# Residual and square ahead of the last weight split, in two output projections and two down projections of a two-layer decoder

## What is computed

```python
for i in range(DEPTH):
    shift, scale, gate = ada_modulation(c, ada_w[i, 0], ada_b[i, 0])
    h = rms_norm(x) * (1.0 + scale) + shift
    y = forgetting_attention(h, ...) if i % 2 == 0 else latent_attention(h, ...)   # ends in  o @ w_o
    x = x + gate * y
    shift, scale, gate = ada_modulation(c, ada_w[i, 1], ada_b[i, 1])
    h = rms_norm(x) * (1.0 + scale) + shift
    x = x + gate * conv_gated_mlp(h, ...)       # ends in  (silu(g) * v) @ w_out
return rms_norm(x) * final_g
```

## Time and profile before

| | |
|---|---|
| median of 3 runs | 1476.24 us (1476.23 to 1476.41) |
| the profiled execution's own time | 1478.92 us |
| its span in the profile | 1477.1 us, 19726 instructions |
| PE busy | 1358.3 us, 92% |
| DVE busy | 837.2 us, 57% |
| ACT busy | 581.3 us, 39% |
| share of engines in the chain that ended last | PE 78%, DVE 8%, issue 6%, ACT 5% |

### The profile page before, as it was taken

The page is one execution under the profiler, slowest core; times in us unless marked ns, Lnnn a source line. Parts: engine busy times, 40 slices in busy tenths (PEclk is TensorE's granted clock), DMA queues, the critical chain, the costliest instruction groups (busy, mean ns, idle before and its releaser), DMA issues.

```text
span 1477.1 us, 19726 instructions
## 1 busy us (share of the span) xinstructions
PE 1358.3 (92%) x6615; PEld 1052.0 (71%) x6615; DVE 837.2 (57%) x1396; ACT 581.3 (39%) x1042; POOL 7.6 (1%) x21
## 2 busy tenths in 40 slices
PE   5799999988999999999988788888879999999997
PEld 2577777655667677888875566666758888888885
DVE  2555666634655556653236578787456666764333
ACT  4444444422422323332223266665344444442222
POOL 2000000000000000000000000000000000000000
PEclk8899999988999999999998799999989999999998
DMA  9521222155466663333331111111213333333331
GB/s 345 187 79 55 58 58 57 30 171 185 168 222 244 223 242 99 99 92 93 94 105 35 22 28 29 30 30 57 71 43 100 99 99 94 92 98 91 105 91 70
DMA packets 224294, 154.70 MB, mean 105 GB/s; under 512 B 28637, under 2 KB 214450, under 8 KB 220146
## 3 DMA queue, kind: packets, MB, share of 16 engines
q1 hardware_dynamic: 224242, 154.01, 33.4%
HBM read 151.89 MB, written 2.10 MB: 104 GB/s over the span
## 4 chain that ended last, share of the span: by engine, by line
PE 78%; DVE 8%; issue 6%; ACT 5%; SPq 1%; DMA 1%; ACTq 0%; DVEq 0%
PE pj L1274 66%; PE ov L1485 2%; PE tr L1452 2%; PE sc L1325 2%; DVE nmax L978 2%; ACT wh L529 1%; PE sc L1435 1%; ACT tmp L616 1%; DMA first_ada<-in_ada_w_dram 1%; PE sc L1331 1%; PE ov L1316 1%; DVE wl L860 1%; DVE tmp L1193 1%; PE ov L1309 1%; ACT tmp L798 1%
## 5 line engine op out<-in xcount | busy, mean ns | idle before, releaser
L1274 PE MATMUL pj<-hh,wh 128*128 128x512 f32 x1000 | 411.5, 411 | 43.4 <-DVE wl L860 10.0
L860 DVE TENSOR_TENSOR wl<-raw,wh 128x1024 fp32r<-128x1024 f32 (+2 forms) x215 | 235.7, 1096 | 375.3 <-ACT wh L529 374.2
L529 ACT ACTIVATE wh<-raw 128x1024 fp32r<-128x1024 f32 (+2 forms) x215 | 205.6, 956 | 526.3 <-PE pj L1274 520.4
L1274 PE MATMUL pj<-hh,wl 128*128 128x512 f32 x1000 | 396.3, 396 | 0.0
L1274 PE MATMUL pj<-hl,wh 128*128 128x512 f32 x1000 | 396.1, 396 | 0.0
L1274 PEld LDWEIGHTS pj<-hh,wh 128*128 128x128 f32 x1000 | 190.9, 191 | 116.8 <-issue 38.2
L1274 PEld LDWEIGHTS pj<-hh,wl 128*128 128x128 f32 x1000 | 191.5, 191 | 42.0
L1274 PEld LDWEIGHTS pj<-hl,wh 128*128 128x128 f32 x1000 | 192.2, 192 | 34.8 <-issue 0.2
L1274 PE MATMUL pj<-gh,wh 128*128 128x512 f32 x512 | 204.3, 399 | 8.3 <-DVE gl L1005 4.3
L1274 PE MATMUL pj<-gh,wl 128*128 128x512 f32 x512 | 201.3, 393 | 0.0
L1274 PE MATMUL pj<-gl,wh 128*128 128x512 f32 x512 | 201.1, 393 | 0.0
(11 more groups left out here) (176 smaller groups left out, 1290.4 us busy)
## 6 DMA issues: line engine op xcount, KB each, us to landing
raw<-in_ffn_w_in_dram SPq DMA_DIRECT2D x88, 512.0 KB, 3.8
ada_w_sb<-in_ada_w_dram SPq DMA_DIRECT2D x36, 1024.0 KB, 6.0
raw<-in_ffn_w_out_dram SPq DMA_DIRECT2D x32, 448.0 KB, 3.8
raw<-in_fox_w_in_dram SPq DMA_DIRECT2D x24, 512.0 KB, 3.8
first_ada<-in_ada_w_dram SPq DMA_DIRECT2D x8, 1024.0 KB, 9.5
raw<-in_ffn_w_out_dram SPq DMA_DIRECT2D x16, 512.0 KB, 4.2
first_ada<-in_ada_w_dram SPq DMA_DIRECT2D x1, 4096.0 KB, 24.0
raw<-in_fox_w_o_dram SPq DMA_DIRECT2D x8, 512.0 KB, 5.5
```

The lines of the kernel that those rows point to most:

```text
L529: act.activation(wh[:, n0 % 2, 0:kt, :], raw[:, n0 % 2, 0:kt, :], ACT.Copy).then_inc(w_hi, 1)
L860: dve.tensor_tensor(wl[:, n0 % 2, 0:kt, :], raw[:, n0 % 2, 0:kt, :], f32(wh[:, n0 % 2, 0:kt, :]), ALU.subtract).then_inc(w_lo, 1)
L1274: ins = pe.matmul(bank_[:, :], (wl if term == 2 else wh)[:, s, kt, :], (rl if term == 1 else rh)(kt), start=start and j == 0, stop=stop an ...
```

## The change

At the written-out end of `dense` (second output tile, `j == 1`) and of `down` (last weight tile, `j == 5`) the residual and its square go ahead of the next weight tile's split, on ACT and on DVE. All other steps keep their order. The instructions and their number stay the same.

```diff
@@ ACT, dense
                 def step(i, j, nxt):
+                    if nxt is not None and j == 1:
+                        residual(i * 2 + j, i * 2 + (T + j), norm_n, j)
                     split_after(C + j, i, 2, nxt)
-                    residual(i * 2 + j, i * 2 + (T + j), norm_n, j)
+                    if nxt is None or j == 0:
+                        residual(i * 2 + j, i * 2 + (T + j), norm_n, j)
@@ ACT, down
                     for j in range(6):
+                        final = nxt is not None and j == 5
+                        if final:
+                            residual(i * 2 + 1, i * 2 + (T + 1), norm_n, 1)
                         if nxt is not None and C + nxt + j + 2 >= C_END:
                             act.wait_ge(mm, C + nxt + j + 1)
                         else:
                             split_after(C + j, i, 6, nxt)
-                        if j % 3 == 2:
+                        if j % 3 == 2 and not final:
                             residual(i * 2 + j // 3, i * 2 + (T + j // 3), norm_n, j // 3)
@@ DVE, dense
                 def step(i, j, nxt):
-                    split_after(C + j, i, 2, nxt)
+                    if nxt is None or j == 0:
+                        split_after(C + j, i, 2, nxt)
                     dve.wait_ge(mm, i * 2 + (C + j + 1))
                     residual(i * 2 + j, j, i * 2 + (T + j), (T + j) % 2, k, norm_n)
+                    if nxt is not None and j == 1:
+                        split_after(C + j, i, 2, nxt)
@@ DVE, down
                     for j in range(6):
-                        split_after(C + j, i, 6, nxt)
+                        final = nxt is not None and j == 5
+                        if not final:
+                            split_after(C + j, i, 6, nxt)
                         if j % 3 == 2:
                             dve.wait_ge(mm, i * 6 + (C + j + 1))
                             residual(i * 2 + j // 3, j // 3, i * 2 + (T + j // 3), (T + j // 3) % 2, k, norm_n)
+                        if final:
+                            split_after(C + j, i, 6, nxt)
```

## The result

The changed kernel took 1464.88 us (median of 6 runs, 1463.45 to 1470.60) beside 1475.99 for the kernel before (6 runs, 1473.97 to 1476.41): a ratio of 0.9932, 95% interval 0.9914 to 0.9949. The profiled execution took 1463.61 with a span of 1461.8.

The account below looks back on a forecast made before the run. TensorE, busy 92%, was taken as the bound, running dry behind products that feed an RMSNorm. Gains of 2.25 + 2.17 + 2.2 = 6.6 us took the median from 1476.24 to 1469.6, range 1466.6 to 1472.9.

Parts of the forecast that it names:

- Three places and not the fourth: Fox output projection, first down projection and MLA output projection gain; the last down projection has no split, so 0.
- the residual at T + 0.03: At three norms, the residual starts within 0.15 of the last product's matmul end, 0.03 in the model row.
- copy, table load and dummy root on the chain: On ACT behind the square, 1.06, 1.28 and 0.20 now precede `stat`, which starts 4.17 after the product's matmuls.
- `wl` hidden ahead of the reciprocal: On DVE, `wl` ends before the reciprocal can start, with 0.2 to spare at fox, 0.6 at the others.
- the moved loads without cost: Tile and modulation loads behind the fox split go out 1.5 later but are wanted over 16 later: 0.
- the next stage moved as a whole: The stage behind each changed norm moves with `stat`: 0 lost; bound 1.45 for each affected tile.
- Rival 1: On ACT, a copy ahead of the table load forces a 1.17 pause; 1.1 gained a place, 1472.9; chance 0.05.
- The rule on a drain: At ACT's table load, a drain makes a switch about 2.66, freeing ACT 1.38 later; 0.87 a place, 1473.6.
- Rivals 2 and 4: Nothing to be had at the norms, 1476.2, chance 0.04; slower by attention-stage half clock, 1479.6 with 20 added, chance 0.03.
- the term that each place gives: `stat` comes earlier by 2.25 at fox, 2.17 at the down projection, 2.2 at MLA's output projection.
- The lower bound T + 4.06: Earliest `stat` after the product's matmuls, with the copy starting 0.54 after the square's start and taking 1.04.
- the mild clock cases of rival 3: Clock falls land elsewhere in the MLA stage and its norm: 1467.0, chance 0.15, or 1471.4 to 1473.1, chance 0.15.

Follow-up runs that it names:

- e6: The changed kernel with ACT put back in the order of before, DVE keeping the new order; median 1466.87 us.
- e7: The changed kernel with the dummy root, which loads the square root's table, moved ahead of the last residual; median 1465.07 us.
- e13: The kernel before plus filler matmuls at four norms, query norm, MLA's first two products, both output projections' entry and ahead of the first modulation rows; median 1467.89 us.
- e4: The kernel before with the change at the fox output projection alone; median 1470.71 us.
- e9: The kernel before with 4 small DVE instructions as pure delay (0.87 us) in the norm behind the fox output projection; median 1473.77 us.
- e1: The changed kernel run once more, unaltered; median 1466.16 us, ratio 0.9941 to the kernel before.

## Why the prediction was right or wrong

**Right: the direction and the mechanism.** Three places and not the fourth; the residual at T + 0.03; copy, table load and dummy root on the chain in place of the mean; `wl` hidden ahead of the reciprocal; the moved loads without cost; the next stage moved as a whole (T1-T2 shrank by 2.61, `stat` came 2.61 earlier). Rival 1 fell: the copy ends at 357.91 and the load starts at 357.93. The rule on a drain in the Trainium skill ("ScalarE: Activation LUTs", "What ACT_TABLE_LOAD costs"), by which 1.38 more would stand there, does not show here either. Rivals 2 and 4 did not come.

**Wrong in size, first: the term that each place gives.** I reckoned 2.25, 2.17 and 2.2, with `stat` at T + 4.17 to 4.26; it came at T + 3.80 to 3.91, so 2.61, 2.63 and 2.52, and 7.8 instead of 6.6. Four parts made the difference. The square begins 0.78 behind the residual's start, as in the earlier trace rows, not 0.92 as in the earlier trace rows, which I had taken as the model. The copy starts 0.54 behind the square, as in the earlier trace rows, the bound that I put aside for the plain sum of durations. `stat` begins 0.09 and 0.10 before the dummy root has ended at the first two places (0.02 behind it at MLA's, hence the 2.52). And the mean ran at full clock at all three places, so ACT alone was the bound. The last was not foreseen: at the down projection I took the clock's fall to stay at 771.0 to 771.5, though all there would come 2.25 earlier. It fell 2.5 behind T before and 5.1 behind T after; in e6 and e7 it fell 2.0 behind T, and the mean took the 1.87 that I had priced.

Of the 2.6 a place, 0.8 is the mean's matmuls at full instead of half clock: with filler and the order of before `stat` stands at T + 5.63 (e13), so the order alone gives 1.8, 1.8 and 1.7 there. (The lower bound T + 4.06 of the prediction adds up to 4.05; nothing hangs on it.)

**Wrong, second, and what put the time outside the range: the mild clock cases of rival 3.** The mechanism was named, but its upper end was set at 1.8 + 0.8, from one attention stage, and a start that could differ was not thought of. Between the two profiles it made 7.3 (5.4 from Tq to T3, 1.8 ahead of T1). The range was said to take both mild cases, yet ended at 1472.9, below the 1473.1 of the second. I also took three runs of before that agreed to 0.2 us as the base, and 0.2% as the noise; 98 executions have a standard deviation of 2.4, so that a single one is uncertain by 4.7 on either side and the mean of six by 1.9. The 4.7 us between the 1469.6 of the forecast and the measured 1464.88 are then: 1.2 from the places, 1.1 because the base of 1476.24 lies above the mean of 1475.1, 1.2 by which the mean of the changed kernel's twelve executions (1466.1) lies below what the places give, and 1.2 because the median of its first six lies below that mean. The base and the last are scatter, that is luck; the third is the part left open below.

**What is shown and what is open.** Shown: 7.8 us belong to the change in the profile, at three places that add up (less where the clock would have fallen late, as at e4's T + 6.06). Shown: stretches with the same instructions differ between executions along with the granted clock, from Tq to T3 by up to 5.8 us across kernels and by 3.2 in one kernel. Not settled: the means of the changed kernels lie 1.2 (all three places, inside its interval) to 1.7 (one or two places, outside theirs) below before by more than the norms give. The profiles from Tq to T3 (252.1 to 252.8 in six with a changed place, more in four of five without) fit the thought that a shorter norm leaves less half clock behind it more often than not. The 251.8 of e9, with the order of before, shows that it needs no change of order, and eleven profiles can't settle it: the cause of this part stays open.

## What to carry to other kernels

Where a chain across engines ends a stage, the in-order queues must hold nothing ahead of its links that the chain doesn't need; here it was enough to turn the order on DVE. Reckon the new chain from the nearest rows of the same pair of instructions, start to start, not from the sum of their durations. Cut two profiles at the same events before a difference of spans is explained: only the stretches that hold an edit may be put down to it. Filler matmuls in TensorE's waits were worth 6.6 ± 1.7 on the kernel before at the four norms alone and 7.3 ± 1.7 at more places (e13), beside 9.0 ± 1.5 for the reordering; with both and the early table load it was 15.9 ± 1.1. They cost where they don't fit in the wait.

## What the runs showed of the hardware

- Where the clock falls differs between executions of one kernel: behind Tq it was at 1.00 until 4.4 us in the first profile of the changed kernel and until 2.9 in the second (e1), and then at 0.50. Across kernels with the same instructions from Tq to T3 it fell 2.5 us behind Tq in the first profile of before and 3.8 behind it in that of e9, and that stage took 257.6 and 251.8. The Trainium skill ("TensorE: Matmul & The Clock Gate", "What's actually happening") calls the monitor behind it free-running; by that rule, the traces agree.
- With that scatter the mean of four executions is uncertain by 1.96 × 2.4 / 2 = 2.4 us, 0.16%.
- ACT can start an instruction that waits for nothing before the last one has ended: the copy 0.09 before the square's end, `stat` 0.09 before that of the dummy root. It does not always: the table load started 0.02 behind the copy's end at all three places, and `stat` at the MLA projection 0.02 behind the dummy root.
